# 192 instead of 160 token copies take V by gathered rows, and POOL forms the products of gates and h

## The reference

```python
def block(args):
    xb, idb, gb = args                     # tokens, 8 heads x 16 picked experts, their gates
    h = jax.nn.gelu(jnp.einsum('td,thkd->thk', xb, u_table[idb]), approximate=False)
    w = (gb * h).astype(xb.dtype)
    return jnp.einsum('thk,thkd->td', w, v_table[idb]).astype(xb.dtype)
```

## Time and profile before

| | us |
|---|---|
| median of three timed runs | 3678.9 |
| the profiled execution | 3670.72 |
| its span | 3668.9 |
| TensorE busy | 3526.7 (96% of the span) |
| DVE busy | 2854.4 (78%) |
| ACT busy | 1196.6 (33%) |
| POOL busy | 1739.4 (47%) |

### The profile page before, as it was taken

How to read it: one execution, slowest core, us unless ns; L and a number is a source line. 1 busy time by engine, 2 the same in 40 slices (tenths; PEclk the granted TensorE clock), 3 DMA queues, 4 the chain that set the end, 5 groups by cost and what they waited for, 6 DMA issues and landing times.

```text
span 3668.9 us, 62596 instructions
## 1 busy us (share of the span) xinstructions
PE 3526.7 (96%) x25292; PEld 3478.4 (95%) x25292; DVE 2854.4 (78%) x3686; ACT 1196.6 (33%) x1214; POOL 1739.4 (47%) x843
## 2 busy tenths in 40 slices
PE   8999999699899999999999999999999999999996
PEld 7999999699799999999999999999999999999996
DVE  4967869655699987777777777776688888988877
ACT  2332333222322234444444444443222222222223
POOL 3332323143433458878778780001665665665311
PEclk9999999799899999999999999999999999999998
DMA  4222212155324669888888887778799898999862
GB/s 150 73 75 77 79 66 82 71 224 210 131 80 143 197 183 229 230 220 226 230 221 226 230 220 226 228 221 288 272 348 352 346 360 349 344 357 352 348 234 95
DMA packets 466252, 788.23 MB, mean 215 GB/s; under 512 B 78976, under 2 KB 376384, under 8 KB 402384
## 3 DMA queue, kind: packets, MB, share of 16 engines
q1 hardware_dynamic: 337920, 547.99, 45.4%
q0 software_dynamic: 83840, 168.15, 14.5%
q10 hardware_dynamic: 44368, 70.57, 5.2%
HBM read 711.43 MB, written 209.34 MB: 251 GB/s over the span
## 4 chain that ended last, share of the span: by engine, by line
PE 80%; DVE 13%; issue 5%; ACT 1%; POOL 0%; DMA 0%; DVEq 0%; SPq 0%; ACTq 0%; POOLq 0%
PE ps L915 32%; PE ps L697 25%; PE ps L947 20%; DVE yb L1541 2%; DVE y_sp L1869 1%; DVE wl L1852 1%; DVE acc L1846 1%; DVE Wl L1829 1%; PE ps L773 1%; DVE wt L1823 1%; PE ps L823 1%; DVE dist L1429 1%; DVE qe L1460 1%; PE ps L819 1%; PE ps L882 1%
## 5 line engine op out<-in xcount | busy, mean ns | idle before, releaser
L599 POOL TENSOR_TENSOR wl<-wraw,wh 128x2048 fp32r<-128x2048 f32 x88 | 432.6, 4917 | 789.9 <-ACT wh L1026 781.1
L649 POOL DMA_INDIRECT g_scratch<-picks,g_col x384 | 685.0, 1784 | 170.4 <-issue 144.0
L1026 ACT ACTIVATE wh<-wraw 128x2048 fp32r<-128x2048 f32 x216 | 414.0, 1917 | 983.8 <-PE ps L947 740.2
L947 PE MATMUL ps<-Wh,wh 128*128 128x384 f32 x2048 | 688.9, 336 | 17.9 <-DVE Wl L1829 11.2
L947 PE MATMUL ps<-Wh,wl 128*128 128x384 f32 x2048 | 686.5, 335 | 0.0
L947 PE MATMUL ps<-Wl,wh 128*128 128x384 f32 x2048 | 686.5, 335 | 0.0
L915 PE MATMUL ps<-xh,wl 128*128 128x272 f32 x1792 | 518.9, 290 | 0.0
L697 PE MATMUL ps<-xh,wh 128*128 128x272 f32 x2304 | 489.8, 294 | 30.1 <-POOL xl L621 12.9
L915 PE MATMUL ps<-xl,wh 128*128 128x272 f32 x1792 | 516.1, 288 | 0.0
L915 PE MATMUL ps<-xh,wh 128*128 128x272 f32 x1792 | 515.8, 288 | 0.3 <-DVE wl L1755 0.3
L697 PE MATMUL ps<-xl,wh 128*128 128x272 f32 x2304 | 481.4, 291 | 0.0
(11 more groups left out here) (301 smaller groups left out, 7159.2 us busy)
## 6 DMA issues: line engine op xcount, KB each, us to landing
wraw<-in_u_t SPq DMA_DIRECT2D x128, 1024.0 KB, 5.1
v_rows<-in_v_t SPq DMA_DIRECT2D x256, 512.0 KB
wraw<-in_v_t SPq DMA_DIRECT2D x128, 1024.0 KB, 5.9
wraw<-in_w_in SPq DMA_DIRECT2D x40, 1024.0 KB, 5.0
g_scratch<-zeros ACTq DMA_DIRECT2D x32, 768.0 KB, 4.7
h_scratch<-hb ACTq DMA_DIRECT2D x64, 384.0 KB, 8.2
gt<-g_scratch SPq DMA_DIRECT2D x64, 384.0 KB, 7.7
hg<-h_scratch SPq DMA_DIRECT2D x64, 384.0 KB, 8.4
```

The costliest lines, as they stand in the source:

```text
L599: nc.gpsimd.tensor_tensor(wl[:, u], wraw[:, u], f(wh[:, u]), ALU.subtract).then_inc(wlo, 1)
L649: nc.gpsimd.indirect_dma_start(g_elem, bass.IndirectOffsetOnAxis(ap=idx, axis=0), gate, None, compute_op=ALU.add).then_inc(g_put, 16)
L947: ins = mat(out, w[:, u, d * EG + e], m[:, e], start=(begin and e == 0 and w is wh and m is Wh[v]), stop=(end and e == EG - 1 and w is wl))
L1026: go(wh[:, u], wraw[:, u], ACT.Copy).then_inc(whi, 1)
```

## The change

TD falls from 384 to 352, so that SD = 192 tokens are gathered. 128 of them take one partition each as before; the other XB = 64 take two partitions each, which makes 64 slots more instead of 32, and ALL = 192. All tiles of the dense way are 352 instead of 384 tokens wide. The slots are spread over 112 steps from n = 6.

The products hg * gt of groups 1 to 15 move from DVE to POOL, which now has a loop over n like DVE's, and `wt` gets a third buffer. Group 0's products stay on DVE. The fold at the end is done in two halves of 8 matmuls with an add between, since 16 blocks of 64 columns do not fit one PSUM bank. Addresses of some buffers move.

```diff
-TD = 384
+TD = 352
 SD = T - TD
...
-NB = P // TS
+XB = SD - P
+NB = P // XB
...
+        STEP0, STEPS = 6, (NG - 1) * EG - 8
+
+        def slots_at(n):
+            i = n - STEP0
+            return range(i * ALL // STEPS, (i + 1) * ALL // STEPS) if 0 <= i < STEPS else ()
...
+            def w_products(g, q):
+
+                pool.wait_ge(g_in[q], g * 16 + 16)
+                pool.wait_ge(h_in[q], g * 16 + 16)
+                for e in (2 * q, 2 * q + 1):
+                    pool.wait_ge(w_s, g * EG + max(0, e - 2))
+                    nc.gpsimd.tensor_tensor(wt[e % 3][:], hg[:, e], gt[:, e], ALU.mult).then_inc(wp_s, 1)
+
             for s in range(HB):
                 h_gather(s)
-            for s in range(ALL):
-                v_gather(s)
-                if s + HB < ALL:
-                    h_gather(s + HB)
+            for n in range((NG - 1) * EG):
+                if 3 <= n % EG < 7:
+                    w_products(n // EG + 1, n % EG - 3)
+                for s in slots_at(n):
+                    v_gather(s)
+                    if s + HB < ALL:
+                        h_gather(s + HB)
...
-            STEP0, STEPS = EG, (NG - 1) * EG - EG - 2
...
                 if 4 <= m < 8:
                     w_lows(g + 1, (g + 1) % 2, [2 * (m - 4), 2 * (m - 4) + 1])
-                if 3 <= m < 7:
-                    w_products(g + 1, [2 * (m - 3), 2 * (m - 3) + 1])
                 for d in range(2):
                     add_y(n, d)
```

More of the change, by code:

```diff
@@ L61 @@
 AHEAD = 4
-TOPK_TILES = ((0, P), (P, P), (2 * P, P), (T - P, P), (TD, TS))
+TOPK_TILES = ((0, P), (P, P), (2 * P, P), (T - P, P), (TD, XB))
 SPARSE, REST = 3, 4
@@ L284, in program @@
         hg = at("hg", [P, EG, TD], F32, HG)
[L285 to L289, removed]
+        wt = [at(f"wt{v}", [P, TD], F32, S0 + EG * ROWD + v * ROWD) for v in range(3)]
+        assert (EG + 3) * ROWD <= 15520
+        fsum1 = at("fsum1", [P, T], F32, X0)
+        fsum2 = at("fsum2", [P, T], F32, X0 + ROW)
+        fsq = [at(f"fsq{u}", [P, T], F32, X0 + (2 + u) * ROW) for u in range(2)]
         XT = HK * TH * 4
@@ L658, in _ @@
                     for tt in G_TILES:
-                        put(g_idx[:, tt, c:c + 1], picks[:, 0, tt, h, k:k + 1])
+                        n = min(P, TD - TOPK_TILES[tt][0])
+                        put(g_idx[0:n, tt, c:c + 1], picks[0:n, 0, tt, h, k:k + 1])
             pool.wait_ge(ids_s, 1)
@@ L1008, in _ @@
             pe.wait_ge(y_sp_s, 2)
[L1009 to L1012, removed]
+            for j in range(NB):
+                if j:
+                    pe.wait_ge(y_sp_u, 5)
+                for k in range(HK):
+                    ins = mat(ps[:, TURN, k * XB:(k + 1) * XB], y_x[:, (j * HK + k) * P:(j * HK + k + 1) * P], fold[:],
+                              start=True, stop=True)
+                ins.then_inc(y_turn, 1)
+                v_tile(NG - 1, 1, 0, j)
+            v_tiles(NG - 1, 1, 1)
             mean_mm(fsum1, fsum2, 4, n2_st, 1, n2_mm)
@@ L1718, in _ @@
             C.done(ts_(s_h[:], s_w[:], float(SD), s_tok[:], ALU.mult, ALU.add), dve)
-            C.done(ts_(s_h[:], s_h[:], float(TS), None, ALU.add), dve)
+            C.done(ts_(s_h[:], s_h[:], float(XB), None, ALU.add), dve)
             C.done(cp(s_hid[:], s_h[:]), dve)
             def rest(a):
-                return picks[0:TS, a, REST].rearrange("p h k -> p (h k)")
+                return picks[0:XB, a, REST].rearrange("p h k -> p (h k)")
             C.done(stt_(r_f[:], rest(1), float(P), rest(2), ALU.mult, ALU.add), dve)
             cp(r_ids[:], r_f[:])
-            C.done(ts_(r_f[:], r_f[:], float(SD), s_tok[0:TS], ALU.mult, ALU.add), dve)
+            C.done(ts_(r_f[:], r_f[:], float(SD), s_tok[0:XB], ALU.mult, ALU.add), dve)
             C.done(cp(r_hid[:], r_f[:]), dve)
[L1729 to L1732, removed]
+            C.done(tt_(fold[:], ident[:, 0:XB], ident[:, XB:2 * XB], ALU.add), ids_s)
             def flat(a):
@@ L1861, in slot @@
                     else:
-                        C.done(tt_(x_w[:], x_h[:], x_gate[:], ALU.mult), dve)
+                        b = slice(s - SLOTS, s - SLOTS + HB)
+                        C.done(tt_(x_w[:, b], x_h[:, b], x_gate[:, b], ALU.mult), dve)
                 v_.wait_ge(sv_in[s % 3], 16 * (s // 3 + 1))
@@ L1922, in _, with add_rest @@
             v_.sem_inc(y_sp_s, 1)
-            v_.wait_ge(y_turn, 5)
-            a_ = acc[:, :, TD:T - P]
-            C.done(stt_(a_, a_, ALPHA, ps[:, TURN].rearrange("p (k t) -> p k t", k=KT), ALU.mult, ALU.add), dve)
+            def add_rest(j, done):
+                v_.wait_ge(y_turn, 5 + j)
+                a_ = acc[:, j * HK:(j + 1) * HK, TD:T - P]
+                C.done(stt_(a_, a_, ALPHA, ps[:, TURN].rearrange("p (k t) -> p k t", k=HK), ALU.mult, ALU.add), done)
+            add_rest(0, y_sp_u)
             nc.vector.memset(fsum1[:], 0.0)
```

53 lines of the change are left out of this document (23 added, 30 removed).

## The result

| | before | after |
|---|---|---|
| median of five runs each, same chip | 3679.13 us | 3932.71 us (3929.23 to 3937.5) |
| ratio, 95% interval | | 1.069 (1.068 to 1.070) |
| profiled execution, its span | 3670.72, 3668.9 | 3929.23, 3927.4 |
| TensorE busy | 96% | 90% |
| mean length of a group (13 groups, n = 12 to 116) | 68.3 us | 85.9 us |

The account below looks back on a forecast made before the run. TensorE was taken as the bound, with DVE and DMA right behind. Fourteen longer groups +302, group 14's missing slot -8, start +14, other tiles -11 make +297 on 3670.7: 3968, say 3970 us; range 3860 to 4100.

Parts of the forecast that it names:

- The mechanism: At m = 4 to 6, POOL's products wait for DVE's `Wl` with gathers queued behind, so the two-tile lead becomes zero.
- The ring: Closed loop in those steps: `Wl` frees the product's buffer, POOL forms product, issues gather, DVE waits, adds, reaches next `Wl`.
- locked step: Each of m = 4, 5 and 6 in a group; predicted to take 15.7 us instead of 8.49.
- D: DVE's start of such a step; the gather was predicted to be issued 2.2 us later, DVE's add at D + 9.4.
- free part: The other five steps of a group: 1.0 + 9.7 + 24.9 + 6.8 = 42.4 us, from 38.6 to 46.7.
- What products do to DVE: Each POOL product costs a non-idle DVE up to 0.95 us; 27 us in sum, left to the upper bound.
- C: Theory tested by the experiments: POOL's product operation hinders DVE; no size or chance of its own.
- The start: Start of the V stage: group 1's products wait behind POOL's gathers of h; +14 us, between 5 and 25.
- Rival 1: Gathers take 9.9 us, as with three in flight; a group 97.6 us, time 4082 us; chance 0.12.
- Rival 3: TensorE's clock stays low, 1.2 GHz for all tiles after a gap; group 116.5 us, about 4350 us; chance 0.03.
- Rival 2: The gathers' lead is kept: 3600 us at TensorE's pace, 3653 at the DMA's, or no change; chance 0.11.
- The signs: Expected in the profile after: hundreds of us of gather waits, groups about 90 us, TensorE busy at 88% or less.

Follow-up runs that it names:

- wait alone: 192-slot kernel with products on DVE, but POOL keeps the products' waits for `Wl` ahead of its gathers, forming nothing; 3918.31 us, ratio 1.065.
- seven or four buffers: Changed kernel, products still on POOL, with seven or four product buffers (`wt`) instead of three; seven 3745.89 us, 1.0185; four 3759.64 us, 1.0217.
- half the adds: 192-slot kernel with products on DVE, adding only 1024 of 2048 columns of each slot after a sum's first (measurement only); 3610.7 us, 0.982.
- products on DVE: Changed kernel with 192 slots and three product buffers kept, products of gates and h moved back from POOL to DVE; 3697.37 us, 1.005.
- gathers first: Changed kernel with POOL's order turned round: in each n the gathers come ahead of the two products, three buffers; 3735.23 us, 1.0152.

## Why the prediction was right, point by point

**The mechanism: right.** The prediction put three steps of each group, m = 4 to 6, behind a wait on POOL's queue. The ring stands in the chain, it arises without any product (wait alone), and it goes when the wait is older (seven or four buffers), when the gathers stand ahead, or when the wait is gone.

**The price of a locked step: too high by 1.4 us.** 15.7 us was predicted, the mean of the 39 locked steps of the 13 groups is 14.3. The mis-sized term is the landing, taken as 7.2 us between the 6.4 of the earlier trace rows and the 7.3 of the earlier trace rows; read from POOL's issue to DVE's start on the row, its mean is 6.2. The chain above has 5.60, 5.63 and 5.66, and 23 of the 39 took 5.5 to 5.8 us. But 12 took 6.8 to 8.1: while these were under way, the queue that loads V, gates and h moved some 1.3 MB, and some 0.4 MB during the 23. One of the 12, on POOL and on DVE:

```profile
3298.04 0.98 POOL L637 DMA_INDIRECT gath<-v_rows,s_ids  x1 [0.15 <-issue]
3305.56 2.35 DVE L1883 SCALAR_TENSOR_TENSOR y_sp<-gath,s_w,y_sp 128x2048 f32<-128x2048 f32 x1 [7.49 <-DMA gath<-v_rows,s_ids]
```

The issue came at D + 1.9 (3187.22 - 3185.32) instead of D + 2.2. Then 1.9 + 6.2 + 2.3 + 2.2, and 2.3 for the second slot in 28 of the 39 steps, make the 14.3. Three steps make 4.2 us, and the free part takes 0.6 back: a group's 89.5 - 85.9 = 3.6. Over all gathers from 2800 to 3400 us:

```profile
L637 POOL DMA_INDIRECT gath<-v_rows,s_ids x97: 938/982/3067, 2799.1 to 3397.9; - x97
...
DMA to landing us min/median/max: 5.5/7.5/11.0
```

**The free part: right in sum, wrong in its working.** 42.4 us was predicted, 43.0 is measured. The prediction let the DMA set 8.3 us a tile; in the chain TensorE ran five tiles, 240 matmuls, in 40.28 us with no gap. At 0.1602 us each that is 38.4, and most of the other 1.9 us are the clock coming back, for which the prediction had 2: the first ten matmuls take 3.05 us (3227.19 to 3230.24) instead of 1.6. The DMA was no bound at 348 GB/s: with half the adds it moved 405. The prediction let TensorE run four tiles and DVE end the part; it runs five. The error of the 8.3 and that of how much of DVE's end shows (2.4 us behind the last of the 240, not 6.8) stand against each other, and that the sum fits is luck. The upper bound of 46.7 us does not add up either: 1.0 + 4 x 9.0 + 6.8 + 1.9 is 45.7. The range does not hang on it.

**What products do to DVE: in the right place.** It was left in the upper bound. In the kernel after, DVE idles where most of them fall, and the groups are as long as with the wait alone (85.9 us both); in the profiled executions the wait alone is 9.2 us faster, 8.5 of them ahead of n = 12. Only when the lead is back do the groups lose 28 to 29 us against products on DVE (gathers first, seven buffers), and C has a part in it. The rule that the prediction cited from the Trainium skill (SBUF — State Buffer, "Who interferes with whom") is borne out by the slots beside a product, 3.18 us against 2.34 with seven buffers.

**The start: the late first `Wl` right, its price too low.** In the time of the profile of before, the first `Wl` of n = 4 was predicted for 2600 us and the `wl` of tile 6 for 2605; less the 7.8 us by which the stage began later they came at 2598.7 and 2604.6. `Wl` waited for a POOL product that stood behind the gathers of h. But to n = 12 the prediction's terms give +6.1 (14, less 12 x 0.66 for narrower tiles), and +17.7 is measured. The larger part of the miss is a misread row. The chain of the kernel before runs ten tiles, from the second on, in one piece:

```profile
2547.89 83.51 PE ps L947 x480
```

So the add at 2556.54 follows the second tile and not the first, and narrower tiles would have brought tile 6 to 2547.9 + 5 x 7.7 = 2586, not 2594. After the change TensorE stood still from 2593.9 to 2612.5, 18.6 us where 11 was predicted. Stretches of the kernel after, in the columns of the earlier trace rows: the gap, tiles 6 and 7, and the next five tiles:

```profile
2594.00:2612.00 18.00, 0.09 (x1) 0.00 (x0) 5.39 (x5) 3.57 (x5) 13.24 (x14) 0.63 0.24 83
2612.50:2630.60 18.10, 17.02 (x97) 16.76 (x97) 10.78 (x15) 6.41 (x7) 11.67 (x10) 0.91 0.89 333
2630.60:2668.80 38.20, 38.20 (x240) 38.16 (x241) 34.25 (x21) 9.33 (x7) 26.45 (x16) 1.00 0.96 378
```

Tiles 6 to 12 take 2.4 us more than 7 x 7.7, for which the prediction had 3. The last 4.6 us are DVE's: it comes to n = 12 2.1 us after TensorE has begun its 14th tile, where before it came 2.5 us ahead of it. Behind it stand gathers that POOL issued late, since the row buffers start empty and beside a busy DVE an issue takes 2 to 3 us. 18.6 + 2.4 + 4.6 - 7.9 = 17.7.

**The narrower matmuls: right in size, worth nothing here.** 0.161 us against 0.1602; but in the groups TensorE was the bound only in the free part.

**The rivals.** Rival 1 (landing of 9.9 us) falls: no landing in a locked step took more than 8.1 us, though its argument, that loads still run, holds in 12 of the 39. Rival 3 (clock stays low) falls by the free part's 0.96. Rival 2 (the lead is kept) did not happen, and the kernels that do keep it did not reach its 3600 to 3653 either: with products on DVE a group takes 69.6 us, since DVE and not TensorE holds it.

**The signs.** One failed: TensorE was to be busy for 88% of the span or less, and is for 90%. Busy time counts the longer matmuls at the lower clock too, so it rose from 3526.7 to 3538.6 us with narrower tiles.

The sum, by parts of the stage, predicted and measured: 13 groups +281 and +228.4 (of the 52 us, 5 are the base of 68.3 instead of 67.9 us a group); to n = 12 +6.1 and +17.7; after n = 116 +11.0 (21.6 - 8 - 2.6) and +4.6; ahead of the stage 0 and +7.8. The one large miss is the locked step, and the start, too low, hides a part of it. 3970 against 3932.7 is 37 us, 0.9%, inside the range.

## What to carry to other kernels

On an engine that issues DMAs in order, ask of each new wait ahead of a DMA how old the awaited event is; if it belongs to the step that also needs the data, the full latency goes into every such step, here 16 us a group with all engines under-used. Put DMAs ahead of the waiting work, or give the work one more buffer, before counting what the work itself costs. Count tiles from a row that names them: an event taken for the end of the first tile was that of the second. When work moves from a vector engine to GpSimd, count what it does to DVE's other operations, and spread fixed work over unequal steps only as far as the buffers hold the lead.

## What the runs showed of the hardware

A gather of 128 rows of 8 KB that was issued with no other gather in flight landed after 5.5 to 5.8 us when the loads beside it moved some 0.4 MB meanwhile, and after 6.8 to 8.1 us when they moved 1.3 MB. The median was 9.9 us with three in flight, and 11.2 us with half the adds, where 405 GB/s were moved. A DMA share of 0.91 at 348 GB/s was therefore no limit.

An indirect DMA on POOL is busy for 0.94 us when DVE idles, but 2 to 3 us when it begins during a DVE operation on two SBUF operands of 2048 columns; the median of the gathers is 2420 ns in the earlier trace rows and 982 ns after the change, where many are issued while DVE waits. In the kernel before, DVE and POOL in order of time:

```profile
2648.72 2.35 DVE L1869 SCALAR_TENSOR_TENSOR y_sp<-gath,s_w,y_sp 128x2048 f32<-128x2048 f32 x1
2650.99 2.29 DVE L1852 TENSOR_TENSOR wl<-wraw,wh 128x2048 fp32r<-128x2048 f32 x1
2651.34 2.75 POOL L630 DMA_INDIRECT gath<-v_rows,s_ids  x1 [3.42 <-DVE y_sp L1869]
```

The issue ends 0.8 us after DVE's `wl` has. From 2700 to 3500 us in this trace 141 indirect DMAs began during a slot's add or a `wl`, and every one ended 0.81 to 0.83 us after it; the 38 that began during an add to `acc`, which reads PSUM, took 0.94 or 0.95 us. So the issue waits for the end of DVE's operation; which part of it does is open. DVE loses nothing by it: with seven buffers a slot beside such an issue alone takes 2.34 us, as others do.

The granted clock was 0.60 on average from 3195 to 3200 us (its lower level is 0.5, 1.2 GHz), where TensorE was busy for 2.35 of 5 us after a gap, and in full again from 3205 on. At the lower level matmuls of 352 columns came 0.29 us apart (3227.64 to 3229.99), and 0.16 us right after it.
